# When three chunks of the next layer's input weights are loaded, in a two-layer decoder trunk

## The chip, the cores and the metric

The kernel runs on 1 core of a Trainium2 chip, as one launch. The metric is the device time of an execution in microseconds (us). The engines are TensorE (PE; PEld is its weight load), VectorE (DVE), ScalarE (ACT), GpSimd (POOL) and SyncE (SP), each with its own instruction stream; they are tied by semaphores. Transfers are issued here by SyncE, ScalarE and GpSimd and carried by 16 DMA engines.

## The reference

Two layers (DEPTH = 2) on a sequence of 1024 tokens of width 1024, all float32. Each layer:

```python
u = rmsnorm(x, norm1_g)
proj = u @ w_in                      # 1024 x 2404, split into the inputs of four head groups
...                                  # four kinds of attention, 4 heads of 64 each: oa, ob, oc, od
h = x + concat(oa, ob, oc, od) @ w_o
y = h + hierarchical_moe(rmsnorm(h, norm2_g), ...)   # top-1 group, top-2 of its 8 experts
x = y                                # input of the next layer
```

The mixture of experts gives each token two expert rows, weighted by their gates; the sum of h and the two rows is the next layer's x.

## The kernel before, in words

Each layer is two blocks of the program, and between blocks all engines meet at a barrier. The first block is `project` and `attend`; the second is `route_experts`.

`project` goes over eight tiles of 128 tokens. The input weight w_in (2404 columns) is kept in SBUF in six chunks of 352, 384, 384, 384, 388 and 512 columns (`CHUNKS`, numbered 0 to 5; 1.4 to 2.0 MB each). For a tile, TensorE transposes x (L407), VectorE applies the gain while it copies the result out of PSUM (L568, tile `uT`), and TensorE multiplies with one chunk after the other (L430), in the order chunk 0, chunk 1, transposes of the next tile, chunks 2 and 3, transposes of the latents (L442), chunks 4 and 5, expansion of the latents (L449 to L451). ScalarE finds the norm: square (L470) and root (L473); VectorE takes the reciprocal (L565).

In layer 1, x isn't stored as such. `x_t[j]` holds h, and the two expert rows of each token lie in DRAM (`expert_rows`), written there by GpSimd's scatters (L1643). `load_y` (L345 to L347) brings them as four transfers for a tile: two of 384 KB, two of 128 KB. VectorE adds them to h (`add_rows`, L554 to L560) and signals `x_summed` (`g.xa`). For tiles 0 and 1 the eight transfers are issued by ScalarE at the end of layer 0's `route_experts` (L1932 to L1934), after it has waited for the last scatters (L1929); h of these tiles is still in SBUF. VectorE adds both tiles before it does anything else (L617, L618). For tiles 2 to 7 SyncE issues `load_y` and the load of h (L397, L398), once tile t's `uT` is made, and stores tile t's sum (L392), which layer 1 needs later.

`route_experts` projects the attention output, chooses experts, and then runs 21 units of expert work in a loop of passes (`passes`, `next_round`; in the profiled execution one pass in each layer). It is a loop whose trip count is known only at run time, so semaphores that are raised inside it are waited for with a value held in a register (`wait_alone`). SyncE loads expert weights set by set into six places in SBUF. Several of these overlap the chunks of w_in. As the last units release their places, SyncE loads the next layer's chunks: chunk 5 at unit U−3, chunks 0 and 1 at unit U−2 (L1595 to L1602), and chunks 2, 3 and 4 after the last scatters have landed (L1610 to L1614).

The order of the work is written out by hand: each engine's stream is as the code has it, and a transfer waits behind all that its engine issues before it.

Of the kernel before, what the change touches and what calls it, by code (L numbers as in the profile page):

```python
# [36 lines left out]
NQR, NKV, NROPE, NNOPE = 192, 128, 32, 32  # L37
GW = HEADS * HD
START_LOADS = 16
CHUNKS = (352, 384, 384, 384, 388, 512)  # L40
AUG = HD + 2
BIG = 1e30
# [12 lines left out]
def trunk(nc, ins, consts, scratch, out):  # L55
# [9 lines left out]
    R = NG + E  # L65
    W1D = sum(CHUNKS)
    coff = [sum(CHUNKS[:c]) for c in range(len(CHUNKS))]
    widths = (3 * GW, 3 * GW, 3 * GW, 2 * GW)
# [175 lines left out]
def w_in_chunk(s, c):  # L244
    return s.r_win[:, s.KT * s.coff[c]:s.KT * (s.coff[c] + CHUNKS[c])].rearrange("p (k n) -> p k n", k=s.KT)


def layer_tables(s, layer):

    ins = s.ins  # L250
    gq, gk = ins["qk_gq"][layer], ins["qk_gk"][layer]
    cq, ck = ins["mla_gcq"][layer], ins["mla_gckv"][layer]
    tabs = [(s.gain_lat[:, 0:1], cq[0:128].rearrange("(p o) -> p o", o=1)),
            (s.gain_lat[0:64, 1:2], cq[128:192].rearrange("(p o) -> p o", o=1)),
            (s.gain_lat[:, 2:3], ck.rearrange("(p o) -> p o", o=1))]
    for n, gain in enumerate((gq, gk)):
        tabs.append((s.gain_a[:, HEADS * n:HEADS * (n + 1), :],
                     bcast(gain[0].partition_broadcast(P).unsqueeze(1), [P, HEADS, HD])))
        for j in range(2):
            tabs.append((s.gain_raw[HD * j:HD * (j + 1), MIXERS * n + 1:MIXERS * (n + 1)].unsqueeze(2),  # L260
                         gain[1:MIXERS].rearrange("m (p o) -> p m o", o=1)))
    for dst, name in ((s.sink_b, "sink"), (s.fox_b, "fox_bf")):
        tabs.append((dst[:, :], ins[name][layer].partition_broadcast(P)))
    return tabs
# [18 lines left out]

def load_w_in(sp, s, g, layer, chunks=range(len(CHUNKS))):
    for c in chunks:
        src = s.ins["w_in"][layer].rearrange("(p k) n -> p k n", k=s.KT)[:, :, s.coff[c]:s.coff[c] + CHUNKS[c]]
        sp.dma_start(w_in_chunk(s, c), src).then_inc(g.w_in[c].sem, 16)


def project_signals(s):  # L290
    sig = s.counted
    NT = s.NT
    g = Shared()
    g.w_in = [sig(f"w_in_loaded{c}", 16) for c in range(len(CHUNKS))]
    g.small = sig("layer_tables_loaded", 16 * len(layer_tables(s, 0)))
# [32 lines left out]
def x_loads(s, layer, i):  # L328

    half = s.NT // 2  # L330
    if layer == 0:
        return 16 * (i + 1)
    return 16 * half + (layer - 1) * (64 + 80 * (half - 1)) + 64 + 80 * i
# [10 lines left out]
def load_y(sp, s, g, t):  # L344
    for n, (a, b, place) in enumerate(y_places(s, t)):  # L345
        sp.dma_start(place, s.y_dram[(n // 2 * s.NT + t) * P:(n // 2 * s.NT + t + 1) * P, a:b]).then_inc(
            g.x[t % 2].sem, 16)  # L347


def project(nc, s, g, layer, block):  # L350
# [24 lines left out]
    def blockfn(block):  # L375
        @block.sync
        def _(sp):
            if layer == 0:
                load_w_in(sp, s, g, 0, (0,))
                sp.dma_start(x_t[1], s.x_f[P:2 * P]).then_inc(g.x[1].sem, 16)  # L380
                load_w_in(sp, s, g, 0, range(1, len(CHUNKS)))
            sp.dma_start(w_l[:, 0:GW], ins["mla_wuq"][layer][0:128]).then_inc(g.wl.sem, 16)
            sp.dma_start(w_l[0:64, GW:2 * GW], ins["mla_wuq"][layer][128:192]).then_inc(g.wl.sem, 16)
            sp.dma_start(w_l[:, 2 * GW:2 * GW + 384], ins["mla_wukv"][layer]).then_inc(g.wl.sem, 16)
            for dst, src in late_tables(s, layer):
                sp.dma_start(dst, src).then_inc(g.late.sem, 16)
            for t in range(NT):
                j = t % 2
                if layer > 0:

                    sp.wait_ge(g.xa.sem, g.xa.at(layer - 1, 4 * (t + 1)))
                    sp.dma_start(s.out_f[t * P:(t + 1) * P], x_t[j]).then_inc(g.xs[j].sem, 16)  # L392
                if t + 2 < NT:
                    sp.wait_ge(g.uT.sem, g.uT.at(layer, 2 * (t + 1)))
                    if layer > 0:
                        load_y(sp, s, g, t + 2)
                        sp.wait_ge(g.xs[j].sem, g.xs[j].at(layer - 1, 16 * (t // 2 + 1)))  # L397
                    sp.dma_start(x_t[j], (s.x_f if layer == 0 else s.h_dram)[(t + 2) * P:(t + 3) * P]).then_inc(  # L398
                        g.x[j].sem, 16)

        @block.tensor
        def _(pe):
            def transpose_x(i, j):
                wait_x(pe, i, j)
                xs = x_t[j].rearrange("p (q k) -> p k q", k=KT)
                for k in range(KT):
                    mm = pe.transpose(bk[3 + k // 4][:, (k % 4) * P:(k % 4 + 1) * P], xs[:, k, :], s.ident[:, :])  # L407
                mm.then_inc(g.xT.sem, 1)

            def tile(i, j, last):  # L410
                t = 2 * i + j

                def chunk(c):
                    n = 6 * j + c
                    b = n % 3
                    if layer == 0:
                        pe.wait_ge(g.w_in[c].sem, g.w_in[c].at(layer, 16))
                    elif t == 0:

                        wait_alone(pe, s, g.w_in[c].sem, g.w_in[c].at(pe.snap(s.rounds_done[pe.engine]), 16))  # L420
                    if c == 0:
                        pe.wait_ge(g.uT.sem, g.uT.at(layer, 2 * t + 2))

                    prev = n - 3
                    reads = 7 * (prev // 6) + (prev % 6 + 1) + (1 if prev % 6 >= 4 else 0)

                    if n > 0:
                        pe.wait_ge(g.mo.sem, g.mo.at(layer, 14 * i + reads + 3))
                    for k in range(KT):
                        mm = pe.matmul(bk[b][:, 0:CHUNKS[c]], uT[j][:, k, :], w_ch[c][:, k, :],  # L430
                                       start=(k == 0), stop=(k == KT - 1))
                    mm.then_inc(g.mm.sem, 1)

                chunk(0)
                chunk(1)
                if not last:
                    transpose_x(i + (j + 1) // 2, (j + 1) % 2)
                chunk(2)
                chunk(3)
                pe.wait_ge(g.mo.sem, g.mo.at(layer, 7 * t + 4))  # L440
                for n, (a, b) in enumerate(((0, 128), (128, 192), (192, 320))):
                    mm = pe.transpose(bk[5][0:b - a, n * P:(n + 1) * P], lat[j][:, a:b], s.ident[:, :])  # L442
                mm.then_inc(g.lT.sem, 1)
                chunk(4)
                chunk(5)
                pe.wait_ge(g.lo.sem, g.lo.at(layer, 3 * t + 3))
                pe.wait_ge(g.wl.sem, layer * 48 + 48)
                pe.wait_ge(g.ao.sem, g.ao.at(layer, 4 * t + 1))
                pe.matmul(bk[6][:, 0:GW], latT[j][:, 0, :], w_l[:, 0:GW], start=True, stop=False)  # L449
                pe.matmul(bk[6][:, 0:GW], latT[j][0:64, 1, :], w_l[0:64, GW:2 * GW], start=False, stop=True)  # L450
                pe.matmul(bk[7][:, 0:384], latT[j][:, 2, :], w_l[:, 2 * GW:2 * GW + 384],  # L451
                          start=True, stop=True).then_inc(g.am.sem, 1)

            pe.wait_ge(s.start_loads.sem, START_LOADS)
            transpose_x(0, 0)
            for i in range(NT // 2 - 1):
                tile(i, 0, False)
                tile(i, 1, False)
            tile(NT // 2 - 1, 0, False)
            tile(NT // 2 - 1, 1, True)  # L460

        @block.scalar
        def _(act):
# [65 lines left out]

            act.wait_ge(s.start_loads.sem, START_LOADS)  # L530

# [17 lines left out]
        def _(dve):  # L549
            dve.wait_ge(s.start_loads.sem, START_LOADS)  # L550
            dve.wait_ge(g.gain1.sem, g.gain1.at(layer, 16))
# [91 lines left out]
        def _(pool):  # L643
            wait_alone(pool, s, s.start_loads.sem, START_LOADS)
            wait_alone(pool, s, g.small.sem, g.small.at(layer, g.small.per_pass))
# [809 lines left out]
def route_experts(nc, s, g, layer):  # L1455
# [5 lines left out]
    last_layer = layer == s.L - 1  # L1461
# [77 lines left out]
    with nc.Block() as block:  # L1539
        @block.sync  # L1540
        def _(sp):
# [8 lines left out]
            with passes(sp):  # L1550
# [13 lines left out]

                if not last_layer:

                    for w_in in s.project_sems.w_in:
                        wait_alone(sp, s, w_in.sem, w_in.at(done, 16))

                for c, e in first_loads[:AT_ONCE]:  # L1570
# [38 lines left out]
                    wait_alone(sp, s, g.hb.sem, sp.snap(s.reloads))  # L1609
                for j in range(2):  # L1610
                    wait_alone(sp, s, g.ys[j].sem, g.ys[j].at(done, g.ys[j].per_pass))
                if not last_layer:

                    load_w_in(sp, s, s.project_sems, layer + 1, range(2, len(CHUNKS) - 1))  # L1614
                next_round(sp)

            if last_layer:
# [671 lines left out]
```

## Time and profile before

| | us |
|---|---|
| median of 3 runs | 2016.41 (2016.15 to 2017.31) |
| the profiled execution | 2015.73 |
| its span, first to last instruction | 2013.9 |
| TensorE busy | 1844.5 (92%) |
| VectorE busy | 712.3 (35%) |
| ScalarE busy | 555.0 (28%) |
| GpSimd busy | 327.6 (16%) |
| DMA, whole span | 325.73 MB, mean 162 GB/s |
| mean granted TensorE clock | 0.959 |

The times in the profile count from the span's start. The profile records when each instruction ran, on which engine and from which line; busy time is what instructions took; an idle stretch is put down to what ended it. A transfer has two times: how long its issue held the queue of the engine that issued it (SPq, ACTq), and how long after the start of the issue it had landed. The granted clock is 1.00 at 2.4 GHz and 0.50 at 1.2 GHz. The layers meet at about 986 to 1008 us.

### The profile page before, as it was taken

The numbers are of one execution on the slowest core, as the hardware profiler recorded it, in microseconds if no ns is written. First come the engines' busy times: TensorE is split into PE (matmuls) and PEld (weight loads), VectorE is DVE, ScalarE is ACT, GpSimd is POOL, SyncE is SP. The second block draws the span as 40 slices with busy tenths as digits, with TensorE's granted clock in tenths as the row PEclk, the third lists the DMA queues.
The fourth block names the chain that finished last, engine by engine and source line by source line (L and its number), as shares of the span: only waits on it lengthen the run. The fifth ranks groups of instructions, "written<-read, shape, count | busy, mean of one in ns | idle before, by whom it ended". The sixth has DMA issues, their size and how long they took to land. (4 is left out here: it accounts for less than half of the span.)

```text
span 2013.9 us, 29209 instructions
## 1 busy us (share of the span) xinstructions
PE 1844.5 (92%) x11200; PEld 1013.2 (50%) x11200; DVE 712.3 (35%) x2085; ACT 555.0 (28%) x1313; POOL 327.6 (16%) x372
## 2 busy tenths in 40 slices
PE   7999998999899889998599999899998997999992
PEld 4555555776645443333255555567675554433330
DVE  0111105667634422222212221266764443222214
ACT  2121216665512201111112121266563222111110
POOL 0333321011100011111013332310210000111110
PEclk9999998999999989999899999999999996999996
DMA  7000000002061389999832110100203315899987
GB/s 261 11 21 11 0 26 28 1 2 95 3 257 63 108 330 416 422 418 413 314 114 84 42 53 0 52 1 1 85 12 127 149 62 221 337 421 422 414 363 307
DMA packets 93208, 325.73 MB, mean 162 GB/s; under 512 B 19856, under 2 KB 33808, under 8 KB 76688
## 3 DMA queue, kind: packets, MB, share of 16 engines
q1 hardware_dynamic: 70416, 272.97, 34.8%
q0 software_dynamic: 12096, 33.57, 4.2%
q10 hardware_dynamic: 10560, 17.33, 2.5%
q8 instruction: 91, 1.49, 0.3%
q14 instruction: 45, 0.37, 0.1%
HBM read 295.52 MB, written 38.80 MB: 166 GB/s over the span
## 5 line engine op out<-in xcount | busy, mean ns | idle before, releaser
L430 PE MATMUL banks<-r_win,r_tile 128*128 128x384 f32 (+3 forms) x1536 | 531.3, 505 | 12.3 <-DMA r_win<-in_w_in 7.6
L430 PEld LDWEIGHTS banks<-r_win,r_tile 128*128 128x128 f32 x1536 | 292.7, 192 | 229.7 <-issue 64.1
L1823 PE MATMUL banks<-r_win,r_proj 128*32 128x512 f32 (+2 forms) x1184 | 256.2, 609 | 9.9 <-DVE r_proj L2144 4.3
L1671 PE MATMUL banks<-r_proj,r_tile 128*128 128x512 f32 x512 | 238.3, 607 | 0.2 <-DVE r_proj L2094 0.2
L1100 ACT ACTIVATE r_win<-r_win 128x256 f32<-128x256 f32 (+7 forms) x256 | 177.4, 695 | 27.8 <-DVE r_win L1172 20.8
L1823 PE MATMUL banks<-r_proj 128*32 128x512 f32 (+1 forms) x736 | 155.4, 594 | 8.2 <-DMA r_win<-in_w 3.6
L983 PE MATMUL banks<-r_win 64*128 64x512 f32 (+3 forms) x704 | 137.9, 512 | 19.6 <-DVE r_win L1144 10.3
L1671 PEld LDWEIGHTS banks<-r_proj,r_tile 128*128 128x128 f32 x512 | 93.0, 193 | 94.4 <-issue 93.9
L994 PE MATMUL banks<-fixed,r_win 128*128 128x128 f32 x984 | 132.6, 281 | 7.4 <-ACT r_win L1108 7.3
L994 PEld LDWEIGHTS banks<-fixed,r_win 128*128 128x128 f32 x984 | 106.3, 141 | 51.0 <-issue 44.2
L500 ACT ACTIVATE r_proj<-banks,rx 128x384 f32<-128x384 f32 (+1 forms) x80 | 48.1, 601 | 296.8 <-PE banks L430 296.8
L1011 PE MATMUL banks<-r_win,r_proj 128*64 128x128 f32 x1968 | 127.1, 278 | 1.5 <-DVE r_tile L1237 1.4
L1838 PE MATMUL banks<-r_win,r_proj 128*32 128x512 f32 (+2 forms) x592 | 127.0, 595 | 1.4 <-ACT r_proj L1924 0.8
L1823 PEld LDWEIGHTS banks<-r_win,r_proj 128*32 128x32 f32 (+2 forms) x1184 | 73.1, 119 | 108.3 <-issue 102.7
L2189 DVE SCALAR_TENSOR_TENSOR r_proj<-banks,rs,r_proj 128x256 f32<-128x256 f32 x42 | 20.3, 484 | 290.4 <-ACT r_proj L1919 290.4
L1108 ACT ACTIVATE r_win<-banks 128x512 f32<-128x512 f32 (+1 forms) x148 | 84.6, 571 | 134.6 <-PE banks L994 134.6
L601 DVE TENSOR_SCALAR r_proj<-banks,rl 128x256 f32<-128x256 f32 x16 | 7.7, 484 | 320.9 <-PE banks L451 320.9
L650 POOL TENSOR_TENSOR r_tile<-r_proj 128x512 f32<-128x512 f32 (+1 forms) x64 | 63.2, 987 | 324.3 <-ACT r_proj L500 296.8
L1011 PEld LDWEIGHTS banks<-r_win,r_proj 128*64 128x64 f32 x1968 | 106.3, 137 | 16.2 <-issue 12.4
L1919 ACT ACTIVATE r_proj<-banks,rs 128x256 f32<-128x256 f32 x42 | 19.9, 474 | 303.4 <-PE banks L1823 303.4
L1823 PE MATMUL banks<-r_tile,r_proj 128*32 128x512 f32 (+1 forms) x384 | 100.6, 599 | 0.0
L983 PEld LDWEIGHTS banks<-r_win 64*128 64x128 f32 x704 | 60.9, 195 | 68.0 <-issue 37.2
(229 smaller groups left out, 2113.7 us busy)
## 6 DMA issues: line engine op xcount, KB each, us to landing
r_win<-in_w SPq DMA_DIRECT2D x99, 1024.0 KB, 18.7
r_proj<-in_w SPq DMA_DIRECT2D x60, 1024.0 KB, 21.4
r_tile<-in_w SPq DMA_DIRECT2D x33, 1024.0 KB, 19.1
r_win<-in_w_in SPq DMA_DIRECT2D x6, 1536.0 KB, 18.2
r_proj<-in_w_o SPq DMA_DIRECT2D x2, 4096.0 KB, 13.8
residual<-r_tile ACTq DMA_DIRECT2D x16, 512.0 KB, 2.9
out<-r_tile SPq DMA_DIRECT2D x16, 512.0 KB, 7.7
r_win<-expert_rows SPq DMA_DIRECT2D x16, 512.0 KB, 9.3
```

The lines of the kernel that those rows point to most:

```text
L430: mm = pe.matmul(bk[b][:, 0:CHUNKS[c]], uT[j][:, k, :], w_ch[c][:, k, :], start=(k == 0), stop=(k == KT - 1))
L500: nc.scalar.activation(dst, bk[b][:, 0:(384 if c == 4 else CHUNKS[c])], ACT.Copy, scale=s.rx[:, j, 2:3]).then_inc(g.mo.sem, 1)
L650: nc.gpsimd.tensor_tensor(sqb[:, 512 * m:512 * m + w], pq, pq, ALU.mult).then_inc(g.sq.sem, 1)
L983: mm = pe.matmul(bk[2 * it.j + it.bank + c // 512][:, 0:cw], qT[x][rows, qb * P:(qb + 1) * P], kT[x][rows, at + c:at + c + cw], start=True ...
L994: mm = pe.transpose(bank[:, b * P:(b + 1) * P], weights[st.slot][:, (at + b) * P:(at + b + 1) * P], s.ident[:, :])
L1011: mm = pe.matmul(O[HD * it.j:HD * (it.j + 1), qb % HALF * P:(qb % HALF + 1) * P], pm[st.m][:, it.kb0 + b, v0:v0 + HD], pT[st.i % 2][:, (it ...
L1100: nc.scalar.activation(p, p, ACT.Exp, bias=top, scale=-1.0, accum_out=den[:, x, it.j, it.qb:it.qb + 1]).then_inc(g.ex.sem, 1)
L1108: nc.scalar.activation(pT[st.i % 2][:, at * P:(at + count) * P], ring_bank("w", (st.i, n))[:, 0:count * P], ACT.Copy).then_inc(g.ra.sem, 1)
L1671: mm = pe.matmul(bk[2 * (t % 2) + c][:, :], mix[t][:, k, :], s.w_o[:, k, 512 * c:512 * c + 512], start=(k == 0), stop=(k == KT - 1))
L1823: mm = pe.matmul(bk[2 + j][at, 0:2 * F].rearrange("p (c n) -> p c n", c=2), xT[j][:, k, at], w13[c][:, :, k, :], start=(k == 0), stop=(k = ...
L1838: mm = pe.matmul(bk[6 + b][at, :], hidT[j][:, k, at], w2[c][:, k, 512 * b:512 * b + 512], start=(k == 0), stop=(k == F // P - 1))
L2189: v.scalar_tensor_tensor(out=hid[j], in0=bk[2 + j][:, F:2 * F], scalar=slot_gates[:, col:col + 1], in1=sil[j], op0=ALU.mult, op1=ALU.mult) ...
```

## The change

The loads of chunks 2, 3 and 4 of the next layer leave `route_experts`. They are issued by SyncE at the start of the next `project` block, when the rows of tiles 0 and 1 have landed (`g.x[0]` and `g.x[1]` at `x_loads(s, layer, 0)`). As they are now loaded once in a layer and not once in a pass, TensorE waits for them with a constant, and SyncE's wait at the start of a pass covers only chunks 0, 1 and 5.

```diff
+AHEAD_CHUNKS = (0, 1, 5)
@@ project, SyncE
                 load_w_in(sp, s, g, 0, range(1, len(CHUNKS)))
+            else:
+
+                for j in range(2):
+                    sp.wait_ge(g.x[j].sem, x_loads(s, layer, 0))
+                load_w_in(sp, s, g, layer, [c for c in range(len(CHUNKS)) if c not in AHEAD_CHUNKS])
@@ project, TensorE, chunk(c)
-                    if layer == 0:
+                    if layer == 0 or t == 0 and c not in AHEAD_CHUNKS:
                         pe.wait_ge(g.w_in[c].sem, g.w_in[c].at(layer, 16))
@@ route_experts, SyncE, start of a pass
-                    for w_in in s.project_sems.w_in:
+                    for w_in in [s.project_sems.w_in[c] for c in AHEAD_CHUNKS]:
                         wait_alone(sp, s, w_in.sem, w_in.at(done, 16))
@@ route_experts, SyncE, end of a pass
                     wait_alone(sp, s, g.ys[j].sem, g.ys[j].at(done, g.ys[j].per_pass))
-                if not last_layer:
-
-                    load_w_in(sp, s, s.project_sems, layer + 1, range(2, len(CHUNKS) - 1))
                 next_round(sp)
```

On SyncE, from the last scatters' wait (`expert_rows_stored`) to the first rows of tile 2, the kernel before has:

```order
L287 DMA r_win<-in_w_in 128x8x384 [waits expert_rows_stored1,start_sets]
L287 DMA r_win<-in_w_in 128x8x384
L287 DMA r_win<-in_w_in 128x8x388
L1524 REGISTER_ALU
L1526 TENSOR_LOAD nrounds [waits round_count_steps]
...
L376 UNCONDITIONAL_BRANCH [waits barrier_Pool_Activation_PE_DVE_SP_release]
L382 DMA w_lat<-in_mla_wuq 128x256
...
L392 DMA out<-r_tile 128x1024 [waits x_summed]
L346 DMA r_proj<-expert_rows 128x768 [waits uT_ready]
```

and the changed one (`x_loaded0` and `x_loaded1` are the semaphores of the rows of tiles 0 and 1):

```order
L1531 REGISTER_ALU [waits expert_rows_stored1,start_sets]
L1533 TENSOR_LOAD nrounds [waits round_count_steps]
...
L378 UNCONDITIONAL_BRANCH [waits barrier_Pool_Activation_PE_DVE_SP_release]
L289 DMA r_win<-in_w_in 128x8x384 [waits x_loaded1,x_loaded0]
L289 DMA r_win<-in_w_in 128x8x384
L289 DMA r_win<-in_w_in 128x8x388
L389 DMA w_lat<-in_mla_wuq 128x256
...
L399 DMA out<-r_tile 128x1024 [waits x_summed]
L348 DMA r_proj<-expert_rows 128x768 [waits uT_ready]
```

The three loads have moved past the barrier, behind the two waits, and ahead of all else that SyncE issues in the block. On TensorE, at tile 0 of layer 1 from chunk 1 on, the kernel before has:

```order
L430 MATMUL banks<-r_win,r_tile 128x384 [waits projection_out,w_in_loaded1,start_sets]
L430 MATMUL banks<-r_win,r_tile 128x384 x7
L407 MATMUL banks<-fixed,r_tile 128x128 [waits x_summed]
L407 MATMUL banks<-fixed,r_tile 128x128 x7
L420 ISA
L430 MATMUL banks<-r_win,r_tile 128x384 [waits projection_out,w_in_loaded2,start_sets]
```

and the changed one:

```order
L437 MATMUL banks<-r_win,r_tile 128x384 [waits projection_out,w_in_loaded1,start_sets]
L437 MATMUL banks<-r_win,r_tile 128x384 x7
L414 MATMUL banks<-fixed,r_tile 128x128 [waits x_summed]
L414 MATMUL banks<-fixed,r_tile 128x128 x7
L437 MATMUL banks<-r_win,r_tile 128x384 [waits projection_out,w_in_loaded2]
```

Its order is the same; a register step before each of chunks 2, 3 and 4 is gone.

## Rows read from the trace of the kernel before

**Rows 1.** Busy time by stretch: times, length, engines busy, PE clock, DMA share, GB/s

```profile
985.60:1001.60 16.00, 0.02 (x2) 0.01 (x1) 3.20 (x10) 0.29 (x2) 0.28 (x1) 0.54 0.83 296
1001.60:1008.30 6.70, 1.97 (x9) 1.62 (x9) 3.75 (x7) 2.64 (x4) 0.00 (x0) 0.50 1.06 374
1008.30:1014.10 5.80, 5.80 (x10) 3.44 (x11) 0.00 (x0) 0.00 (x0) 0.00 (x0) 0.50 1.08 375
1014.10:1022.00 7.90, 7.90 (x31) 5.03 (x30) 0.00 (x0) 2.25 (x8) 0.00 (x0) 1.00 0.31 117
```

**Rows 2.** Timeline of TensorE: start, length, what, count [idle before <- released by]

```profile
1001.63 1.95 PE L407 MATMUL banks<-fixed,r_tile 128*128 128x128 f32 x8 [16.00 <-DVE r_tile L560]
1008.28 13.04 PE L430 MATMUL banks<-r_win,r_tile 128*128 128x352 f32 x32 [4.71 <-DVE r_tile L568]
1021.15 1.04 PE L407 MATMUL banks<-fixed,r_tile 128*128 128x128 f32 x8
1022.03 10.49 PE L430 MATMUL banks<-r_win,r_tile 128*128 128x384 f32 x32
...
1032.68 12.24 PE L430 MATMUL banks<-r_win,r_tile 128*128 128x388 f32 x32
```

**Rows 3.** Timeline of VectorE at the same place

```profile
994.96 0.06 DVE L552 MEMSET junk<- 128x1 f32 x1 [5.56 <-PEq L1539]
998.99 2.50 DVE L560 TENSOR_TENSOR r_tile<-r_tile,r_proj 128x768 f32<-128x768 f32 x4 [3.97 <-DMA r_proj<-expert_rows]
1004.38 2.50 DVE L560 TENSOR_TENSOR r_tile<-r_tile,r_proj 128x768 f32<-128x768 f32 x4 [2.90 <-DMA r_proj<-expert_rows]
1006.79 0.15 DVE L565 RECIPROCAL rx<-rx 128x1 f32<-128x1 f32 x1
...
1024.59 2.49 DVE L560 TENSOR_TENSOR r_tile<-r_tile,r_proj 128x768 f32<-128x768 f32 x4
...
1046.86 0.48 DVE L601 TENSOR_SCALAR r_proj<-banks,rl 128x256 f32<-128x256 f32 x1 [19.71 <-PE banks L451]
```

**Rows 4.** Timeline of ScalarE (ACTq: its DMA issues)

```profile
989.58 4.37 ACTq L346 DMA_DIRECT2D r_proj<-expert_rows  x8
...
1001.51 1.06 ACT L470 ACTIVATE r_tile<-r_tile 128x1024 f32<-128x1024 f32 x1 [6.14 <-DVE r_tile L560]
...
1003.98 0.29 ACT L473 ACTIVATE rx<-rx,eps 128x1 f32<-128x1 f32 x1
```

**Rows 5.** Timeline of SyncE's issues; the first line merges six chunks

```profile
954.82 38.82 SPq L287 DMA_DIRECT2D r_win<-in_w_in  x6
...
1004.24 0.47 SPq L392 DMA_DIRECT2D out<-r_tile  x1
1008.16 1.75 SPq L346 DMA_DIRECT2D r_proj<-expert_rows  x4
1012.15 0.32 SPq L398 DMA_DIRECT2D r_tile<-residual  x1
```

**Rows 6.** Line 287, from 988 to 989.9: issues of chunks 2 to 4, landing

```profile
L287 SPq DMA_DIRECT2D r_win<-in_w_in x3: 540/662/3752, 988.6 to 989.9; - x3
...
DMA to landing us min/median/max: 8.7/16.1/19.9
```

**Rows 7.** Line 346, from 985 to 1000: landing of tiles 0 and 1

```profile
DMA to landing us min/median/max: 6.0/8.4/10.9
```

**Rows 8.** Line 346, from 1020 to 1400: landing of tiles 3 to 7

```profile
DMA to landing us min/median/max: 2.9/3.5/5.4
```

**Rows 9.** DMA queues from 990.5 to 1000 (q1 SyncE's, q10 ScalarE's): packets, MB, share

```profile
q1 hardware_dynamic: 1404, 2.13, 61.9%
q10 hardware_dynamic: 745, 1.47, 41.5%
```

**Rows 10.** Line 287, from 0 to 20, at the program's start: landing

```profile
DMA to landing us min/median/max: 7.9/25.4/26.7
```

**Rows 11.** Timeline of TensorE, chunks 0 and 1 of a later tile

```profile
1188.29 10.06 PE L430 MATMUL banks<-r_win,r_tile 128*128 128x352 f32 x32
```

## The prediction

> **What bounds the kernel now.** The place to read is the boundary between the two layers, so I began with the busy time by stretch [rows 1]. In the 16.0 us from 985.6 to 1001.6 TensorE is busy 0.02 us. In the next 6.7 it has only eight transposes, and from 1008.3 to 1014.1 it is busy throughout but at clock 0.50. The DMA engines show the opposite: a share of 1.06 and 1.08 in the last two. The kernel is a chain on TensorE here: the first product of layer 1 starts at 1008.28 [rows 2], and work then follows work with no gap that the row shows.
>
> What ends the idle time is read backwards. The product waits for the second tile's rows, though it only needs the first: on VectorE both additions (998.99 and 1004.38, 2.50 us each) stand ahead of the reciprocal at 1006.79 and of the copy that the product wants [rows 3]. Each addition waited for DMA. VectorE had entered the block at 994.96, so 4.0 us were lost ahead of the first, and 1004.38 − (998.99 + 2.50) = 2.9 us between the two. ScalarE's part for tile 0, square, table load and root, runs 1001.51 to 1004.27, which is 2.76 us, beside the second addition [rows 4].
>
> Why the rows come late: ScalarE issues eight row loads (2.1 MB) from 989.58 to 993.95 [rows 4], while SyncE has just issued three weight chunks (4.7 MB) from 988.6 on [rows 6]. The row loads take 6.0 to 10.9 us to land [rows 7]; the same loads for later tiles take 2.9, 3.5 in the median, 5.4 at most [rows 8]. In 990.5 to 1000 the weights' queue moved 2.13 MB and the rows' queue 1.47 MB [rows 9]. Tile 0 had to let about as much weight through as it brought itself.
>
> **The change part by part.**
>
> *Three loads leave the stretch 988.6 to 1004.* The waits for the scatters, the eight row issues and the block's barrier stay. The last SyncE issue ended at 954.82 + 38.82 = 993.64 [rows 5], ScalarE's at 993.95, so ScalarE holds the barrier and its release stays at about 994.9. Landing: ScalarE's eight issues take 4.37 us, 0.55 each, so tile 0's last goes out near 991.2 and tile 1's near 993.5. No row shows eight such loads alone. The near bound is the median of later ones, 3.5 us (landed 994.7 and 997.0); the far one is their slowest, 5.4 (996.6 and 998.9). I take 4.0, as eight queue behind each other more than four do: 995.2 and 997.6. The bytes agree: 2.1 MB at the 3.60 MB in 9.5 us of [rows 9], 0.38 MB a us, is 5.5 us from about 991.
>
> *The chain from there.* First addition 995.2 to 997.7, second 997.7 to 1000.2. ScalarE's 2.76 us begin at 997.7 and end at 1000.5, and so become the later of the two by 0.3. From the reciprocal's start to the product were 1008.28 − 1006.79 = 1.49 us, so the product starts at 1002.0 instead of 1008.28: **6.3 us earlier**. With the far bound it is 996.6, 999.1, root 1001.9, product 1003.4: 4.9 us. With the near one the barrier decides (995.0, 997.5, root 1000.3, product 1001.8): 6.5 us. If ScalarE's issues also go at the 0.44 us that SyncE's take for the same loads (1.75 us for four, [rows 5]), the barrier moves 8 × 0.11 = 0.9 us more: 7.4 us.
>
> *The cold start stays.* Chunks 0 and 1 take 13.04 us here [rows 2] and 10.06 at clock 1.00 [rows 11], so 2.98 us go to the lower level. TensorE is idle before the product in both kernels; I carry this over, at zero change. The granted clock rises at the end of [rows 1]'s fourth row, 5.8 us after the product's start.
>
> *Do the three chunks come in time?* SyncE now issues them when both tiles' rows have landed, at 997.6, 0.6 us apart. Before, they landed 8.7, 16.1 and 19.9 us after issue [rows 6], with 2.1 MB of rows beside them; even at that they are in at 1006.3, 1014.3 and 1018.8. Chunk 2 is wanted 1022.03 − 1008.28 = 13.75 us after the product's start, at 1015.8; chunk 3 half of 10.49 us later, at 1021.0; chunk 4 at 1032.68 − 6.3 = 1026.4 [rows 2]. The cover is 9.5, 6.7 and 7.6 us: cost nothing. On SyncE's queue 4.7 MB without the rows should be in by about 997.6 + 2 + 4.7/0.38 = 1012 (estimate, from rows 9 and the 2 us or so before first bytes in the fastest landing of rows 8).
>
> The Trainium skill speaks against this edit: DMA: Bandwidth & Descriptors, Rules for kernel authors, says to issue a load early and wait on it late. The trace agrees that nothing of the three loads is waited for when early, but here what they hold back is wanted sooner. By the rule the sum would be zero or a loss; by rows 7 and 8 it is the 6.3 us.
>
> *SyncE's queue behind the moved loads.* Behind them stand three expansion weights, three small tables, the store of tile 0, tile 2's rows and residual. Before, the store was issued 1004.24 − 988.6 = 15.6 us after the first chunk, and the residual, which waits for the store's landing, 7.9 us after the store [rows 5, 6]. At the same distances now: store 1013.2, rows 1013.7, residual 1021.1, landed at 1026.5 with the 5.4 us of rows 8. VectorE's addition for tile 2 would start at 1024.59 − 6.3 = 1018.3, so it may wait up to 8 us and end by 1029. Behind it VectorE has nothing that TensorE wants before the copy at 1046.86 − 6.3 = 1040.5 [rows 3]. So 11 us of cover; if it went, each us more would be paid on TensorE.
>
> *Small things.* On SyncE three of six waits at the start of the expert pass go; on TensorE three register steps before chunks 2 to 4, hidden under running products. Both nothing: they stand before loads that are issued long before use. Bounds: 0 to 0.3 us gain.
>
> **The sum.** Only the boundary changes; after it, TensorE's work and the transfers are released by each other, so I let all of it shift. The profiled execution: 2015.73 − 6.3 = 2009.4. As the first landings are the least certain term and lean to the late side, I take 6.0: 2009.7. The median of the runs stands 0.7 us above that execution (2016.41), so by the median it is 2010.4; I forecast 2010.0.
>
> **Rivals.**
>
> *The clock does not come up with the work* (the gain is halved). It fell during the idle stretch and rose at 1014.1. If it rose there whatever the start, the product would run 12.1 us at the lower level instead of 5.8, and 6.3/2 = 3.15 of the gain go: 2012.6. For it: TensorE's eight transposes at 1001.6 did not bring the clock up [rows 1, 2], so what counts as work is narrow. Against: only one rise is seen, and it came after continuous products. On this the Trainium skill (TensorE: Matmul & The Clock Gate, Part 1) says that the window runs freely and isn't started by a kernel's first product; by that the 2.98 us could come out smaller or larger in any execution, before and after alike. The trace has one such start at this place and can't show the spread.
>
> *The rows land no sooner, or what is won is lost again.* If the eight loads were slow for themselves, from the scatter just before or from their issue on ScalarE, they land at 998.9 and 1004.4 as now, and the chunks go out at 1004.4, in by about 1025.6 at their present 19.9, wanted at 1032.7. Gain 0, time 2015.7. For: no later row load has eight in a row. Against: the queues' shares in rows 9.
>
> *Slower: chunk 2 comes too late.* It decides once chunk 2 lands after 1022.0, that is 24.4 us after issue. The slowest chunk of the whole trace took 26.7 us [rows 10], in the queue at the program's start. At that it lands at 1024.3, 2.3 us later than TensorE's turn now, and an idle stretch of 8 us would bring the low clock once more, another 2.98: 2015.7 + 2.3 + 2.98 = 2021. Against: chunk 2 is first in an empty queue.
>
> *It doesn't do what it says:* a stray early release is excluded by the order of instructions, where the three loads wait for both tiles' loads. No chance of its own.
>
> **How the numbers follow.** The likeliest case 0.75, its own range 2008 to 2011.5 (gains 7.4 to 4.9, with the 0.7 between execution and median). Clock rival 0.08, no gain 0.12, slower 0.05. From no change 0.2% (4 us) can be told. The first case is faster; the clock rival and the no-gain case are within: faster 0.75, same 0.20, slower 0.05. The range reaches to the clock rival's 2013.3 by the median and leaves the last two out: 2007.3 to 2013.8.
>
> **What would show it.** In the changed profile: the two additions following each other without a DMA wait over 1 us, from about 995; row loads landing in 3 to 5.5 us; the reciprocal released by ScalarE's root; the product at about 1002; chunks landed by 1012 and no DMA wait ahead of chunk 2; TensorE at clock 0.50 for about 6 us. Wrong would be: rows still 6 to 11 us in landing, a wait for the input weights on TensorE, or a low-clock stretch of 12 us. If VectorE's addition for tile 2 waits more than 8 us, the queue term was mis-sized.

## The result, and the profile after

The changed kernel's median is 2004.82 us (2002.86 to 2005.41, 4 runs) against 2016.28 (2015.35 to 2017.31, 4 runs): ratio 0.995, 95% interval [0.9932, 0.9969]. It is faster, as forecast, but by 11.5 us where some 6 were forecast (2010.0), and the time lies below the range. Two more comparisons (below) gave 7.2 and 9.0 us: together, 15 runs of the changed kernel have a median of 2005.4, 32 of the one before 2014.8, a gain of 9.4 us (95% interval 7.0 to 10.7, by resampling these times). The profiled execution took 2005.33 us, its span 2003.5.

Busy time by stretch at the boundary, the columns as in [rows 1]:

```profile
983.80:997.10 13.30, 0.02 (x2) 0.03 (x1) 3.23 (x11) 0.31 (x2) 0.28 (x1) 0.56 0.58 191
997.10:1001.30 4.20, 1.97 (x9) 1.60 (x9) 3.81 (x7) 2.62 (x4) 0.00 (x0) 0.50 0.67 211
1001.30:1005.80 4.50, 4.50 (x8) 2.75 (x9) 0.00 (x0) 0.00 (x0) 0.00 (x0) 0.50 1.08 383
1005.80:1013.50 7.70, 7.70 (x26) 4.63 (x26) 0.00 (x0) 1.60 (x6) 0.00 (x0) 1.00 0.98 331
```

The idle stretch is 13.3 us where [rows 1] had 16.0, the one with the transposes 4.2 for 6.7, the cold one 4.5 for 5.8. The DMA share in the idle stretch, 0.83 before, is 0.58. TensorE's timeline, answering [rows 2]:

```profile
997.10 1.95 PE L414 MATMUL banks<-fixed,r_tile 128*128 128x128 f32 x8 [13.29 <-DVE r_tile L567]
1001.27 12.37 PE L437 MATMUL banks<-r_win,r_tile 128*128 128x352 f32 x32 [2.23 <-DVE r_tile L575]
1013.49 1.05 PE L414 MATMUL banks<-fixed,r_tile 128*128 128x128 f32 x8
1014.37 10.49 PE L437 MATMUL banks<-r_win,r_tile 128*128 128x384 f32 x32
```

The product starts 7.0 us earlier, but layer 0 had already ended 1.8 us earlier. Chunk 2 follows without a wait. VectorE and ScalarE, answering [rows 3, 4]:

```profile
992.04 0.06 DVE L559 MEMSET junk<- 128x1 f32 x1 [4.46 <-PEq L1546]
994.46 5.10 DVE L567 TENSOR_TENSOR r_tile<-r_tile,r_proj 128x768 f32<-128x768 f32 x8 [2.36 <-DMA r_proj<-expert_rows]
999.78 0.17 DVE L572 RECIPROCAL rx<-rx 128x1 f32<-128x1 f32 x1 [0.22 <-ACT rx L480]
...
1023.38 2.50 DVE L567 TENSOR_TENSOR r_tile<-r_tile,r_proj 128x768 f32<-128x768 f32 x4 [6.37 <-DMA r_tile<-residual]
```

```profile
987.76 3.71 ACTq L348 DMA_DIRECT2D r_proj<-expert_rows  x8
...
996.99 1.06 ACT L477 ACTIVATE r_tile<-r_tile 128x1024 f32<-128x1024 f32 x1 [4.53 <-DVE r_tile L567]
...
999.45 0.29 ACT L480 ACTIVATE rx<-rx,eps 128x1 f32<-128x1 f32 x1
```

The additions of both tiles are now one group of eight, with no wait between them, and the reciprocal is released by ScalarE's root, 0.22 us after VectorE was free. The eight issues take 3.71 us for 4.37. The addition for tile 2 waits 6.37 us, and nothing on TensorE waits for it. Landing of the rows (line 348, from 985 to 1000) and of the three chunks (line 289, from 985 to 1010), answering [rows 7] and [rows 6]:

```profile
DMA to landing us min/median/max: 2.8/5.1/6.0
```

```profile
DMA to landing us min/median/max: 6.7/11.7/16.1
```

SyncE's issues, answering [rows 5]:

```profile
1008.45 0.48 SPq L399 DMA_DIRECT2D out<-r_tile  x1
1008.97 2.48 SPq L348 DMA_DIRECT2D r_proj<-expert_rows  x4
1017.51 0.32 SPq L405 DMA_DIRECT2D r_tile<-residual  x1
```

### The profile page after: what moved, and what is told of

Its sections match the earlier page's. It is cut to its first block and busy times, and to the rows that moved or that the text cites. A ratio compares the mean times of both kernels' runs of the same rounds, so it can differ in the third digit from the quotient of the medians.

```text
span 2003.5 us, 29201 instructions
## 1 busy us (share of the span) xinstructions
PE 1841.7 (92%) x11200; PEld 1013.5 (51%) x11200; DVE 712.4 (36%) x2085; ACT 555.0 (28%) x1313; POOL 327.6 (16%) x372
## 3 DMA queue, kind: packets, MB, share of 16 engines
q10 hardware_dynamic: 10560, 17.33, 2.5%
q8 instruction: 91, 1.49, 0.3%
## 5 line engine op out<-in xcount | busy, mean ns | idle before, releaser
L1018 PEld LDWEIGHTS banks<-r_win,r_proj 128*64 128x64 f32 x1968 | 105.8, 137 | 16.1 <-issue 12.2
```

The costliest lines, as they stand in the source:

```text
L1018: mm = pe.matmul(O[HD * it.j:HD * (it.j + 1), qb % HALF * P:(qb % HALF + 1) * P], pm[st.m][:, it.kb0 + b, v0:v0 + HD], pT[st.i % 2][:, (it ...
```

## The experiments

The stretches of every trace, in us, worked out from the starts of TensorE's products, so that a gap here is some 0.2 us longer than the idle time in brackets in a row of the profile. "Boundary" runs from the last product of layer 0 to the first of layer 1; "rise" from that one to the clock's rise; "chunks" from the first product to the start of the latents' transposes, with chunks 0 to 3 in between; "gather" is the gap before the first transposes of layer 1's experts, which wait for a gather.

```
trace                        layer 0  boundary  rise  chunks  gather   span
before                        985.4    22.85    5.9   24.08    3.3   2013.9
before again (e2)             982.0    22.83    5.8   24.04    3.5   2012.0
changed                       983.6    17.65    4.5   23.42    2.1   2003.5
changed again (e1)            984.4    17.23    4.6   23.45    2.5   2007.0
changed third (e5)            983.6    17.10    5.1   23.70    2.4   2003.4
e3 loads after the loop       985.4    21.55    3.5   22.90    4.0   2011.0
e4 no row wait                985.8    17.08    4.6   23.47    4.6   2009.6
e6 table and order            982.7    16.19    5.9   24.08    2.9   2005.5
e7 table early                981.7    17.18    5.1   23.67    3.1   2001.7
e10 table early again         984.1    16.80    5.0   23.64    2.3   2006.7
e8 rows split                 982.2    19.13    6.0   24.16    2.5   2007.5
e9 before, table and order    984.6    19.71    5.2   23.73    3.6   2009.2
e11 no row wait, t. and o.    986.5    16.79    5.2   23.74    4.3   2009.5
e12 delay                     982.8    18.07    3.8   23.03    2.5   2002.3
e13 dummy waits               984.6    18.01    4.4   23.35    2.3   2005.0
e14 gather first              980.2    17.18    3.4   22.87    0.2   1999.1
e15 all three                 978.5    16.31    6.0   24.12    0.2   1999.3
```

**e1, e2, e5: both kernels again.** No edit.

> The changed kernel once more, for a second trace and more times. In the first pair of profiles the boundary gave 5.9 us (first product and chunks 0 and 1 of layer 1, less what layer 0 was ahead already), 1.8 us were ahead before the boundary and 2.8 us came after it. Theory A (only the boundary is the change's doing, the rest is where the clock happens to fall and rise and other variation between executions): boundary again 5 to 7 us, the other two parts differ by 1 us or more from the first pair, and the median gain over more runs drifts down towards 6 to 9 us. Theory B (the rest is the change's doing too): the same 1.8 and 2.8 us within 0.5, and a gain of 10.5 to 12 us again.

> The kernel before once more, for a second trace. Theory A: its marks (last product of layer 0, first product of layer 1, start of the experts of layer 1) lie up to 2 us away from those of its first trace, though nothing is changed. Theory B: they repeat within 0.5 us.

> The changed kernel a third time, with more runs of both. So far the stretch from the last product of layer 0 to the first of layer 1 took 22.8 us in both traces before and 17.7 and 17.2 in both of the change; layer 0 alone varied from 982.2 to 985.6 us with nothing changed. Theory A (the change is worth the boundary and what follows from it there, 6 to 7 us; the 11.5 of the first comparison had up to 5 us of variation in layer 0 and in the experts): median gain 5 to 9 us, boundary 17.0 to 17.7, layer 0 again anywhere in 982 to 986. Theory B (a second effect of 5 us that belongs to the change): gain over 9.5 us.

Measured: e1 2007.27 us (5 runs) against 2014.45 (17 runs), 0.9964 [0.995, 0.9977]; e5 2005.47 (6 runs) against 2014.45 (11 runs), 0.9954 [0.9941, 0.9967]; e2 one run, 2013.77. The boundary repeats within 0.02 us in the two traces before and 0.55 in the three of the change: 22.84 to 17.33, 5.5 us, and the chunks behind it take 0.5 less (24.06 to 23.52). That is 6.0 us in all. Layer 0 is 3.4 us apart in the two traces of the one unchanged kernel, more than the 2 that theory A allowed, so the 1.8 us that the first pair shows ahead of the boundary say nothing of the change. So far theory A; but the pooled gain is 9.4 us, and some 3 us more remained to be looked for. They are not certain: the lower bounds of the three comparisons are 4.6 to 6.6 us.

**e3: past the barrier or not.** The loads leave the start of `project`, with the wait for the rows, and stand behind the loop, still ahead of the barrier:

```diff
                 next_round(sp)
+            if not last_layer:
+                load_w_in(sp, s, s.project_sems, layer + 1, [c for c in range(len(CHUNKS)) if c not in AHEAD_CHUNKS])
```

> The three loads are issued by SyncE right after the loop over passes, ahead of the barrier, so still beside the row loads; everything else of the change stays (constant waits on TensorE, three waits fewer on SyncE at the start of a pass). Theory A: the boundary is as before within 1 us, time 2015 to 2017. Theory B in the form that the small edits matter: 3 to 6 us faster than before, 2010 to 2013.

Measured: 2010.90 us (11 runs), 0.9986 [0.9977, 0.9995], some 3 us faster than before. VectorE:

```profile
997.23 0.06 DVE L554 MEMSET junk<- 128x1 f32 x1 [8.02 <-PEq L1541]
997.97 2.50 DVE L562 TENSOR_TENSOR r_tile<-r_tile,r_proj 128x768 f32<-128x768 f32 x4 [0.68 <-DMA r_proj<-expert_rows]
1003.09 2.50 DVE L562 TENSOR_TENSOR r_tile<-r_tile,r_proj 128x768 f32<-128x768 f32 x4 [2.62 <-DMA r_proj<-expert_rows]
```

The wait for tile 1's rows is back (2.62, before 2.90), and the last load's issue (up to 5.8 us) now holds the barrier. The boundary, 21.55, is 1.3 us shorter than before and the chunks 1.2, as the clock rose 3.5 us after the product. Theory A expected the boundary within 1 us and the time at 2015 to 2017: the boundary is a little off, and the time is 4 us below it, in the 2010 to 2013 of theory B. Boundary and chunks together are 2.5 us shorter than before in this trace; the rest of the gain is not assigned. Most of the boundary's gain (4.2 of 5.5 us) goes with the loads' place; e3 drops the wait for the rows as well, and e4 shows that this is not what lengthens the boundary.

**e4: the explicit wait.** The change without its two lines `for j in range(2): sp.wait_ge(g.x[j].sem, ...)`.

> The three loads are issued at the start of the next block as in the change, but SyncE does not wait for the rows. They go out at about 993 instead of 996.5, when the row loads are under way. If the block's barrier alone gives the rows their lead: tile 0's rows land as in the change, tile 1's 1 to 2 us later, and since the root of ScalarE takes as long as the second addition, the first product comes 0 to 1.5 us later than in the change: 1 us slower than it at most. If the explicit wait is what matters (rows held back by whatever weight loads are in the queues): tile 1's rows land 3 us later or more, and 2 to 4 us are lost against the change.

```profile
994.09 0.06 DVE L557 MEMSET junk<- 128x1 f32 x1 [4.46 <-PEq L1544]
995.93 2.50 DVE L565 TENSOR_TENSOR r_tile<-r_tile,r_proj 128x768 f32<-128x768 f32 x4 [1.78 <-DMA r_proj<-expert_rows]
998.96 2.50 DVE L565 TENSOR_TENSOR r_tile<-r_tile,r_proj 128x768 f32<-128x768 f32 x4 [0.53 <-DMA r_proj<-expert_rows]
```

Boundary 17.08, as with the wait: the barrier gives the rows all the lead they need, and the wait for them only holds tile 2's rows back (6.37 us of waiting on VectorE, here 1.05). Yet the time is 2009.45 (7 runs), 0.9975 [0.9963, 0.9986], 2.2 us more than e1 in the same comparison; the intervals overlap, and the boundary can't be the reason. In the trace layer 0 is 1.9 us longer than the change's mean (983.9), which is within what the unchanged kernel varies by, and the gather's gap is 2.3 us longer. It led to e13.

**e6, e7, e10: what limits the boundary now.** e7 and e10 are the change with ScalarE's first activation a root, so that its table is loaded early; e6 has VectorE's order too:

```diff
-            nc.scalar.activation(s.junk[:, 1:2], s.eps[:, 0:1], ACT.Copy).then_inc(g.mo.sem, 3)
+            nc.scalar.activation(s.junk[:, 1:2], s.eps[:, 0:1], ACT.Sqrt).then_inc(g.mo.sem, 3)
...
             if layer > 0:
                 add_rows(0, 0)
-                add_rows(0, 1)
             evac_x(0, 0)
+            if layer > 0:
+                add_rows(0, 1)
```

> The change, and besides: ScalarE's first activation of the block is a square root, so the table is loaded before the rows are in, and VectorE makes tile 0's operand before it adds tile 1's rows. If the chain from tile 0's rows is add, square, root, operand, product, as read from the change's trace, 1.28 us of table load leave it and the second addition no longer stands in it: boundary 16.0 us (1.2 to 1.4 less). If tile 1's rows or the barrier hold it, nothing changes. On the whole time that is 1 us, less than this comparison tells; the boundary stretch of the trace tells it.

> The change with the early table load alone. In the change the second addition ended only 0.2 us before ScalarE's root, so the two chains are about equal: taking 1.28 us from one should give 0.2 us and no more (boundary 17.0). If ScalarE's chain alone were the limit it would give 1.3.

> The change with the early table load, once more and timed. Boundary 17.0 to 17.3 as in its first trace. If whole times beyond the boundary only vary by execution, the median is within 3 us of the change's 2005.4 on either side; the single 2003.6 was luck.

Measured: boundary 16.19 in e6 (1.1 less than the change's mean), 17.18 and 16.80 in e7 and e10 (0.15 and 0.5 less): the two chains were about equal. But the chunks of e6 took 24.08 for 23.52, as the clock rose 5.9 us after the product; half the boundary's gain went there. e6 took 2008.07 us (6 runs), 0.9966 [0.9954, 0.9978]; e7 2003.55 in its one run and e10 2008.38 (5 runs), 0.9961 [0.9947, 0.9974]: nothing of e7's low time was the edit's; the single run was luck.

**e8: rows issued by two engines.** SyncE issues tile 1's rows behind the loop, ScalarE only tile 0's.

> The change, with tile 1's row loads issued by SyncE, beside tile 0's on ScalarE. ScalarE's issues no longer hold the barrier for 3.7 us but for 1.9. If the barrier limits, VectorE enters the block 1.5 us or more sooner; but the first addition waited 2.2 us for tile 0's rows after the barrier, and with both tiles' loads sharing the DMA engines from the start these land later, by up to 1.5 us. Expected: barrier 1.5 us sooner, first addition 0 to 1.5 us later, boundary 17.2 to 18.7, so no gain.

```profile
989.12 0.06 DVE L559 MEMSET junk<- 128x1 f32 x1 [2.56 <-PEq L1546]
994.53 4.91 DVE L567 TENSOR_TENSOR r_tile<-r_tile,r_proj 128x768 f32<-128x768 f32 x8 [5.36 <-DMA r_proj<-expert_rows]
```

VectorE waited 2.56 us at the barrier for 4.46, and then 5.36 us for tile 0's rows for 2.36: boundary 19.13, 1.8 us worse and 0.4 more than the worst expected. In this trace tile 0's last rows landed 6.4 us after their issue, for 5.4 in the change, with tile 1's rows issued beside them instead of behind them. The Trainium skill (DMA: Bandwidth & Descriptors, Issuing engines are not separate DMA queues) says that transfers issued by several engines interleave on the same 16 DMA engines; the trace agrees: when tile 0's rows were in, so were tile 1's, and the eight additions have no wait between them.

**e9: the reading of the trace before.** The kernel before, with both edits of e6.

> The kernel before (three loads early, as they were), with ScalarE's table loaded early and VectorE making tile 0's operand before it adds tile 1's rows. If the trace before was read rightly (tile 0's rows landed 13.4 us after the last product of layer 0, and the product waited 2.9 + 2.5 us more for tile 1's rows and their addition), the product needs tile 0's rows, 2.5 us of addition, 1.5 of square and root and 1.5 to the product: boundary 13.6 + 5.6 = 19.2 us instead of 22.8, 3.6 less without moving a load. Chunks 2 to 4 are early enough. If the first rows are slow for another reason than the weight loads, nothing else changes either way.

```profile
998.25 2.50 DVE L560 TENSOR_TENSOR r_tile<-r_tile,r_proj 128x768 f32<-128x768 f32 x4 [4.26 <-DMA r_proj<-expert_rows]
1002.28 0.17 DVE L565 RECIPROCAL rx<-rx 128x1 f32<-128x1 f32 x1 [1.54 <-ACT rx L473]
...
1004.08 2.49 DVE L560 TENSOR_TENSOR r_tile<-r_tile,r_proj 128x768 f32<-128x768 f32 x4
```

Boundary 19.71 (19.2 expected), 3.1 us shorter without moving a load; 2010.95 us (11 runs), 0.9985 [0.9976, 0.9994]. So over half of the 5.5 us that the change wins at the boundary was to be had by both edits together. Neither was run alone on the kernel before. By the rows the order alone would give some 2.4 us (an estimate: without the early table the root ends at 1000.75 + 2.76 = 1003.5 and the product starts 1.49 later, at 1005.0 for 1004.3); that much was the wait for tile 1, which the first product never needed.

**e11: no wait, and both edits of e6.**

> The change without the wait for the rows, with the early table load and tile 0's operand first. Tile 1's rows, which the loads hold back, are no longer in the chain, so the wait should be worth nothing here: boundary 16.0 to 16.4 as with the wait, and VectorE's addition for tile 2 waits 1 us instead of 6. Median 2004 to 2009.

Measured: boundary 16.79 (0.4 over the expected), addition for tile 2 waiting 0.94 us, 2010.02 us (11 runs), 0.9971 [0.9961, 0.9981]. Again a kernel without the wait is at 2010, outside what was expected. Whole times don't separate the two kinds, though: e6 and e10, which have the wait, are at 2008, and layer 0 of e11's trace is 2.6 us longer than the change's mean.

**e12: the clock.** The change, with one multiplication of 1152 columns on VectorE ahead of tile 0's operand.

> The change with one idle multiplication of 1152 columns on VectorE after both additions, into a buffer not yet in use: 1.3 us by the additions' 1.22 us for 1000 columns, so the first product comes 1.1 us later (boundary 18.2 to 18.8). If the clock rises at the time it would have risen anyway, the first two chunks lose less time at the low clock and their stretch is 0.5 us shorter (22.9 to 23.1); if the rise follows the product, it stays 23.4 to 23.7.

```profile
1000.87 11.99 PE L437 MATMUL banks<-r_win,r_tile 128*128 128x352 f32 x32 [3.78 <-DVE r_tile L575]
```

The product came 0.7 us later (18.07, below the 18.2 to 18.8 expected), the rise 3.8 us after it for 4.7 in the mean of the change, and the chunks took 23.03 for 23.52 (23.42 to 23.70 in its three traces). The granted clock was 0.50 for 20.5 us here, as in all three traces of the change: the rise did not move with the product, and 0.5 of the 0.7 us came back.

It is one trace, and e14 weakens it: with the boundary of the change (17.18), the 20.5 us at 0.50 and no delay in the boundary, its rise came 3.4 us after the product and its chunks took 22.87, as the clock fell sooner (0.1 us after the start of layer 0's last product, for 1.3 to 1.7 in the change). So that a delay of the product gives time back is not shown beyond what an execution does by itself.

Over all traces the rise came 3.4 to 6.0 us after the product, never the 12 of the clock rival. The Trainium skill (TensorE: Matmul & The Clock Gate, Part 1) says that the window which the gate watches runs freely and does not begin anew with a kernel, so that the clock's change comes at a varying distance from the first product; the traces agree, by the 3.4 to 6.0 us.

**e13: the place of instructions in SyncE's stream.** The change with two waits that are long fulfilled in place of the row wait:

```diff
                 for j in range(2):
-                    sp.wait_ge(g.x[j].sem, x_loads(s, layer, 0))
+                    sp.wait_ge(s.start_loads.sem, START_LOADS)
```

> The change without the row wait, but with two waits in its place that are long fulfilled (on the start loads), so SyncE's stream has the same instructions as in the change. In the traces so far SyncE issues its first expert load of layer 1 after GpSimd's first gather 0.70 us later in the eight kernels with the row wait and 0.37 us in the six without it, and TensorE's wait for that gather was 2.1 to 3.1 us in the first and 3.3 to 4.6 in the second. Theory P (the place of instructions in SyncE's stream does this, not the row wait): distance 0.70 us, wait 2.1 to 3.1 us, boundary 16.8 to 17.7, median 2004 to 2008 like the change. Theory W (something that follows from the row wait): distance 0.37, wait 3.3 to 4.7, median 2009 to 2011 as the kernel without any wait.

In layer 1's `route_experts` SyncE issues two expert sets just after GpSimd's first gather of token rows. The gather, SyncE's next issue, and TensorE's first use, in the kernel before:

```profile
1693.35 1.08 POOL L1636 DMA_INDIRECT r_proj<-residual,rs  x1 [13.52 <-DVE rs L2082]
```

```profile
1693.71 0.83 SPq L1558 DMA_DIRECT2D r_win<-in_w  x2
```

```profile
1701.71 1.97 PE L1807 MATMUL banks<-fixed,r_proj 128*128 128x128 f32 x8 [3.05 <-DMA r_proj<-residual,rs]
```

in e4:

```profile
1686.70 1.08 POOL L1638 DMA_INDIRECT r_proj<-residual,rs  x1 [13.53 <-DVE rs L2084]
```

```profile
1687.07 1.14 SPq L1563 DMA_DIRECT2D r_win<-in_w  x2
```

```profile
1696.37 1.97 PE L1809 MATMUL banks<-fixed,r_proj 128*128 128x128 f32 x8 [4.36 <-DMA r_proj<-residual,rs]
```

and in e13:

```profile
1684.99 1.08 POOL L1640 DMA_INDIRECT r_proj<-residual,rs  x1 [12.01 <-DVE rs L2086]
```

```profile
1685.69 0.82 SPq L1565 DMA_DIRECT2D r_win<-in_w  x2
```

```profile
1692.34 1.97 PE L1811 MATMUL banks<-fixed,r_proj 128*128 128x128 f32 x8 [2.05 <-DMA r_proj<-residual,rs]
```

From gather to SyncE's issue are 0.36, 0.37 and 0.70 us, and the wait is 3.05, 4.36 and 2.05. Theory P holds: waits that wait for nothing give the change's distance and its short gather. Over the traces before e14 the two kinds do not overlap: a gap of 2.1 to 3.1 us at the distance of 0.70, of 3.3 to 4.6 at 0.37. The time, 2007.33 (6 runs), 0.9963 [0.9948, 0.9977], agrees, but its interval overlaps that of e4 and decides nothing; the boundary (18.01) was 0.3 over what was expected. So the change won about 1.1 us here (mean gap 3.4 before, 2.3 in the change) by two instructions more in SyncE's stream and not by what they wait for. e3 and e4 have the three waits fewer and the moved loads of the change, but not these two, and are at 0.37.

**e14, e15: the same mechanism where the change did not touch it.** SyncE waits for the first gather before it issues those two sets; e15 adds both edits of e6.

```diff
                 sp.wait_ge(g.hs.sem, g.hs.at(layer, 16 * NT))
+                wait_alone(sp, s, g.gx[0].sem, g.gx[0].at(done, 16))
                 for c, r in first_loads[AT_ONCE:]:
```

> The change, and SyncE issues the two expert sets that follow the gathers only when the first gather has landed. From issue of the gather to the first product on it are 7.2 to 9.7 us in both layers now, with 2.1 to 4.6 us of waiting on TensorE. If the gather is slow because of the expert loads beside it, as the rows were, it lands 3 to 5 us after its issue; TensorE then waits for nothing here, 4.1 us less in layer 0 and 2.3 us less in layer 1: median 1999 to 2002. If the sets come too late instead, TensorE waits for them in the first units and the gain is smaller or gone. If the gather is slow by itself, nothing changes but the sets come later.

> The gather first, and ScalarE's table and tile 0's operand early. Boundary 16.2 us, waits for the gathers as in the kernel with the gather first alone: 1 us faster than it, within what this comparison tells; 1998 to 2002.

Measured: e14 2001.60 us (6 runs) against 2013.61 (11 runs), 0.9938 [0.9924, 0.9952]; e15 2000.67 (6 runs), 0.9933 [0.9919, 0.9947]. TensorE's first use of the gather in layer 0, in the change and in e14:

```profile
710.05 1.97 PE L1811 MATMUL banks<-fixed,r_proj 128*128 128x128 f32 x8 [3.87 <-DMA r_proj<-residual,rs]
```

```profile
705.16 1.97 PE L1812 MATMUL banks<-fixed,r_proj 128*128 128x128 f32 x8
```

And the gathers' landing in layer 0, in the change (line 1640, from 700.5 to 703) and in e14 (line 1641, from 699 to 702):

```profile
DMA to landing us min/median/max: 9.1/9.7/10.4
```

```profile
DMA to landing us min/median/max: 4.4/4.8/5.1
```

The waits are gone in both layers (gap 0.2): the gather was slow because of the expert loads beside it. Not all of it is won. The gaps were 4.2 and 2.3 us in the mean of the change's traces, but the rest of the experts' work behind them takes longer in e14, 275.0 us for 273.4 in layer 0 and 314.6 for 312.4 in layer 1 with the tail; there TensorE waits 7.2 and 7.7 us for expert weights, in the change's traces 5.6 to 6.6 and 5.8 to 6.5. The medians differ by 3.8 us from the change's, or by 2.6 when each is set against the kernel before. e15 is the fastest kernel of the study, 13 us under the one before; that it beats e14 is not shown.

## Why the prediction was wrong

**Right: the mechanism, and the boundary's size.** Rows were late because of the weight loads beside them (e3 puts the loads back, and the wait is back); with these gone they land in 2.8 to 6.0 us (bounds 3.5 and 5.4 for each tile's last; tile 0's last took 5.4, tile 1's 6.0). The additions close up, the reciprocal waits for the root, as written. The boundary gave 5.5 us for 6.3 (6.0 taken, far bound 4.9). The difference is tile 0's landing, taken at 4.0 us after its last issue: in the first pair the first addition began 10.8 us after layer 0's last product where the sum has 9.8. The barrier came sooner (8.4 us after that product for 9.5), but VectorE then waited 2.36 us for the rows, so this gave nothing.

**Wrong but small: "the cold start stays".** It shrank by 0.5 us, as the clock rose 4.5 to 5.1 us after the product and not 5.8. (The prediction puts the rise before at the end of [rows 1]'s fourth row; it is the end of the third, at 1014.1.)

**Right: the chunks come in time.** They landed 6.7 to 16.1 us after issue, the last at 1014.5 and not by 1012, and nothing waited; SyncE's queue made VectorE wait 6.4 us for tile 2, within the 8 allowed and without a price.

**The step that failed: "only the boundary changes; after it, ... I let all of it shift".** It put the rest of the program at zero and gave it no bounds. Two things stood there. First, an effect of the change outside the boundary. The two waits that it adds in front of the chunks were counted for what they wait for, and as instructions at nothing; for the small edits I had "0 to 0.3 us". As instructions, they moved SyncE's issue by 0.33 us against a gather some 700 us later, and that was worth 1.1 us (e13). The three waits fewer and the moved loads did not do it (e3, e4). Second, what an execution varies by: layer 0 alone by 3.4 us in two traces of one kernel, and the medians of the kernel before by 2.7 between comparisons (2016.28 to 2013.61). The first comparison's 11.5 us hold 6.0 of the boundary and the chunks behind it, 1.1 of the gather, and 4.4 that are not assigned; its two traces have 1.8 us of such a difference in layer 0. By all 15 runs the gain is 9.4, and 2.3 are left, which the interval of 7.0 to 10.7 does not tell from none. In the traces 0.9 of these stand in layer 1's attention and router (clock rises at other points), 0.4 in the tail; whether these belong to the change is open. So the terms that were priced came out near their size; the time lies below the range by the unpriced gather and by a rest whose cause stays open.

**Sums and readings.** The sum gives 2010.4 by the median, and I wrote 2010.0. The likeliest case's own range, with gains of 7.4 to 4.9, is 2009.0 to 2011.5 by the median and not from 2008. Tile 0 did not let "about as much" weight through as it brought: from 989.5 to 999 the weights' queue moved 2.0 MB, and tile 0 is 1.05. None of these moves the range to the measured time.

**The rivals.** "No sooner", "chunk 2 too late" and the clock rival's 12 us at the lower level did not occur. That a shift of the product against the clock's rise takes or gives time is seen in single traces (e12, e14) and shown for no edit; and no run tested whether "what counts as work is narrow". That the explicit wait was needed, which I took for granted when I issued the chunks "when both tiles' rows have landed", is refuted by e4: passing the barrier does it.

## What to carry to other kernels

Large loads that nobody waits for yet cost time when a small transfer on the critical chain runs beside them; look wherever a wait for a small transfer is much longer than the same transfer takes elsewhere in the trace, and hold the large ones until it has landed. Then ask what the first consumer really needs: over half the boundary's gain was to be had without moving a load, by ordering VectorE's work and loading ScalarE's table early. Before a difference of a few us is explained, take two traces of the same kernel and see which stretches repeat (here the boundary, to 0.02 us) and which don't (layer 0, 3.4 us).

## What the runs showed that was not expected

- Two fulfilled waits in SyncE's stream, some 700 us ahead, moved its issue in a later block by 0.33 us (e13 against e4). The distance from the gather was 0.37 us in all six traces without them and 0.70 in all nine with a wait there (e14 and e15, which move the issue itself, are not counted). Why is not shown.
- A third of a microsecond of lead went with 1 to 2 us less of waiting for a gather of one unit's token rows beside the expert loads; a lead of 5.4 us or more (e14) removed the wait for it.
- The clock's rise came 3.4 to 6.0 us after the first product of layer 1, within 0.1 us the same in both traces before (5.86, 5.81), 4.5 to 5.1 in three traces of the change, and 3.4 in e14 with the same boundary. The chunks behind it took 22.9 to 24.2 us accordingly, which is as large as some edits' effect.
